# Nine column groups of the adaptive modulation: partition sums moved from TensorE to VectorE's 32x32 transpose and row sums

## The reference

```
sc  = silu(c);  scc = silu(c_ctx)
mod_l = sc  @ ada_w[i] + ada_b[i]        # 6 x 1024 values for the latent tokens
mod_c = scc @ ada_w[i] + ada_b[i]        # 6 x 1024 values for the context tokens
sh1, s1, g1, sh2, s2, g2 = split(mod, 6)
```

## Time and profile before

| | |
|---|---|
| median of 3 runs | 1933.3 us (1932.83 to 1934.34) |
| the profiled execution | 1933.96 us, its span from first to last instruction 1932.1 us |
| mean granted TensorE clock | 0.999 |
| PE busy | 1921.8 us, 99% of the span |
| PE weight loads busy | 1653.0 us, 86% |
| DVE busy | 1371.3 us, 71% |
| ACT busy | 674.7 us, 35% |
| POOL busy | 381.2 us, 20% |

### The profile page before, as it was taken

The page is one execution under the profiler, slowest core; times in us unless marked ns, Lnnn a source line. Parts: engine busy times, 40 slices in busy tenths (PEclk is TensorE's granted clock), DMA queues, the critical chain, the costliest instruction groups (busy, mean ns, idle before and its releaser), DMA issues.

```text
span 1932.1 us, 24878 instructions
## 1 busy us (share of the span) xinstructions
PE 1921.8 (99%) x9432; PEld 1653.0 (86%) x9432; DVE 1371.3 (71%) x1977; ACT 674.7 (35%) x936; POOL 381.2 (20%) x364
## 2 busy tenths in 40 slices
PE   9999999999999999999999999999999999999998
PEld 6889899899889988998888888888888888888887
DVE  3756587698887777767887755754764787777778
ACT  2423122145323222331546225324413443434443
POOL 0300312313211222222310130130030037110004
PEclk9999999999999999999999999999999999999999
DMA  9623334345998998898596285366447525977656
GB/s 327 262 70 67 120 121 131 106 135 134 210 230 216 215 230 231 229 236 226 175 223 240 88 251 181 129 192 197 151 144 231 173 90 178 246 210 194 175 146 148
DMA packets 120419, 350.59 MB, mean 181 GB/s; under 512 B 17520, under 2 KB 30448, under 8 KB 115568
## 3 DMA queue, kind: packets, MB, share of 16 engines
q1 hardware_dynamic: 91200, 268.11, 40.9%
q0 software_dynamic: 27280, 77.08, 22.2%
q10 hardware_dynamic: 1824, 3.85, 0.6%
HBM read 296.01 MB, written 40.92 MB: 174 GB/s over the span
## 4 chain that ended last, share of the span: by engine, by line
PE 95%; POOL 1%; DMA 1%; DVE 1%; issue 1%; ACT 0%; SPq 0%; POOLq 0%; DVEq 0%; ACTq 0%
PE bank L1157 18%; PE bank L1159 18%; PE bank L1158 18%; PE bank L1195 4%; PE bank L1196 4%; PE bank L1197 4%; PE bank L1565 3%; PE bank L1564 3%; PE bank L1562 3%; PE bank L1626 3%; PE bank L1627 3%; PE bank L1624 3%; PE bank L1809 2%; PE bank L1808 2%; PE bank L1806 2%; PE bank L1468 1%
## 5 line engine op out<-in xcount | busy, mean ns | idle before, releaser
L2377 DVE TENSOR_TENSOR w_lo<-raw,w_hi 128x1024 fp32r<-128x1024 f32 x132 | 168.8, 1282 | 170.8 <-ACT w_hi L1832 170.6
L1832 ACT ACTIVATE w_hi<-raw 128x1024 fp32r<-128x1024 f32 x132 | 139.2, 1055 | 279.3 <-PE bank L1159 158.9
L1157 PE MATMUL bank<-w_hi,act_hi 128*128 128x512 f32 x504 | 198.2, 393 | 0.0
L1159 PE MATMUL bank<-w_hi,act_lo 128*128 128x512 f32 x504 | 196.4, 390 | 0.0
L1158 PE MATMUL bank<-w_lo,act_hi 128*128 128x512 f32 x504 | 196.3, 390 | 0.0
L1157 PE MATMUL bank<-hT_hi,w_hi 128*128 128x384 f32 (+2 forms) x544 | 191.8, 353 | 0.0
L1158 PE MATMUL bank<-hT_lo,w_hi 128*128 128x384 f32 (+2 forms) x544 | 190.8, 351 | 0.0
L1159 PE MATMUL bank<-hT_hi,w_lo 128*128 128x384 f32 (+2 forms) x544 | 190.8, 351 | 0.0
L1195 PE MATMUL bank<-w_hi,hT_hi 128*128 128x512 f32 x336 | 131.0, 390 | 0.0
L1196 PE MATMUL bank<-w_lo,hT_hi 128*128 128x512 f32 x336 | 130.8, 389 | 0.0
L1197 PE MATMUL bank<-w_hi,hT_lo 128*128 128x512 f32 x336 | 130.7, 389 | 0.0
(11 more groups left out here) (458 smaller groups left out, 4858.2 us busy)
## 6 DMA issues: line engine op xcount, KB each, us to landing
raw<-w_units_d SPq DMA_DIRECT2D x234, 512.0 KB, 4.6
mod<-mod_units_d SPq DMA_DIRECT2D x64, 384.0 KB, 4.5
wsum<-w_units_d SPq DMA_DIRECT2D x44, 512.0 KB, 4.5
raw<-weight_sums_d SPq DMA_DIRECT2D x32, 512.0 KB, 4.4
wsum<-w_units_d POOLq DMA_DIRECT2D x25, 512.0 KB, 7.9
wsum<-wsum POOLq DMA_DIRECT2D x19, 512.0 KB, 7.0
bv<-mod_units_d SPq DMA_DIRECT2D x16, 512.0 KB, 3.6
weight_sums_d<-w_units_d POOLq DMA_DIRECT2D x8, 1024.0 KB, 12.4
```

The costliest lines, as they stand in the source:

```text
L1157: nc.tensor.matmul(out, s_hi, m_hi, start=first, stop=False)
L1159: return nc.tensor.matmul(out, s_lo, m_hi, start=False, stop=last)
L1832: nc.scalar.activation(halves_of(phase, k, i)[0], raw[:, s, :], ACT.Copy).then_inc(hi_done, 1)
L2377: tt(lo, raw[:, s, :], f32(hi), ALU.subtract).then_inc(lo_done, 1)
```

## The change

In the nine places the sum over partitions goes to DVE. `nc.vector.transpose` transposes every 32x32 block of the tile by itself, so that in each quarter of 32 partitions a row sum over 32 neighbouring values is the sum over the quarter's 32 partitions for one column. Two instructions for each 128x1024 tile (`part_sum`): the transpose into a scratch tile, and a `tensor_reduce` to 128x32; in the MLP each tile goes in two halves of 384 columns. TensorE then adds the four quarters and sets the sums in their partitions with four small matmuls (`part_columns`): the weights are `sel32`, four 32x32 unit matrices one under another (made once, in `v`), the moving operand has 16, 12 or 6 columns, and each writes 32 partitions of bank 7. DVE adds the bias from there (`add_part_bias`).

The places move. `vz`: DVE sums between its first and second `split_lo`, TensorE's matmuls where the transposes were. `gmlp`: DVE sums between the last two `split_lo` of `down`, that is behind the drains of half 0; TensorE's matmuls behind the second tile of the last sweep; the bias behind DVE's second drain of half 1. `ffn0`: DVE sums in one place behind `products(4)`; TensorE's matmuls behind the fifth tile of the last sweep; the bias behind the fifth drain of half 1. Step `rows` and ACT's copy are gone in all nine. The first product of the next group waits for DVE's own count `small_done` in place of TensorE's step.

```diff
-_VZ = _V[:2] + [("rows2", 6, "A")] + _V[2:3] + [("cols2", 7, "D")] + _V[3:]
+_VZ = _V[:3] + [("cols2", 7, "D")] + _V[3:]
-_DOWN0M = _DOWN0[:1] + _ROWS + _COLS + _DOWN0[1:]
+_DOWN0M = _DOWN0[:10] + _COLS + _DOWN0[10:]
-_DOWN0S = _DOWN0[:8] + _ROWS + _DOWN0[8:10] + _COLS + _DOWN0[10:]
+_DOWN0S = _DOWN0[:13] + _COLS + _DOWN0[13:]
...
+            def part_columns(phase, i, label, n, vectors):
+                sums = part_sums_v if phase == "vz" else part_sums
+
+                pe.wait_ge(small_done, sums_made(phase, i))
+                free(phase, i, label)
+                for q in range(4):
+                    src = sums[:, 0:vectors, 0:4 * n].rearrange("p v (j q) -> p q j v", q=4)[:, q]
+                    last = nc.tensor.matmul(bank[7][32 * q:32 * q + 32, 0:n * vectors].rearrange("p (j v) -> p j v", v=vectors),
+                                            sel32[:, :], src, start=True, stop=True, tile_position=(0, 32 * q))
+                last.then_inc(pe_step, 1)
...
                 token_units(phase, i, 0, "v", TILES0, {} if phase == "v" else {
-                    (1, 5): sums_2, (2, 5): lambda: mod_columns("vz", 0, 2, rbuf[:, 0, :], 7)})
+                    (2, 5): lambda: part_columns(phase, i, "cols2", 8, 2)})
...
-                    down(phase, i, CH, TILES0, act_hi0, act_lo0, ready, rows=rows, columns=columns)
+                    down(phase, i, CH, TILES0, act_hi0, act_lo0, ready,
+                         columns1=lambda: part_columns(phase, i, "cols0", 8, 2))
...
-                    down(phase, i, 7, TILES0, act_hi0, act_lo0, ready, rows1=rows, columns1=columns)
+                    down(phase, i, 7, TILES0, act_hi0, act_lo0, ready, after=TILES0 - 2,
+                         columns1=lambda: part_columns(phase, i, "cols0", 6, 2 if p < PIECES_MIXED else 1))
...
-                    mod_rows(phase, i, 0, rows1[:, 0:6] if p >= PIECES_MIXED else rows1[:, :], 6, begin)
...
                     products(4)
+                    group1_sum(p, 0)
+                    group1_sum(p, 1)
+                    group1_sum(p, 2)
+                    group1_sum(p, 3)
                     block0_lo(p + 1, 0)
                     drain0(p, 1, 0)
                     drain0(p, 1, 1)
-                    mod1_columns(phase, i)
                     for t in range(2, TILES0 - 1):
                         drain0(p, 1, t)
                         products(5, t - 2)
+                    add_part_bias(phase, i, "cols0", 1, 6 * i, 6, 2 if p < PIECES_MIXED else 1)
...
+            def part_sum(done, v, a, src, turned, sums=part_sums):
+
+                n = src.shape[1] // 32
+                dve.wait_ge(small_done, done)
+                nc.vector.transpose(turned, src).then_inc(small_done, 1)
+                dve.wait_ge(small_done, done + 1)
+                nc.vector.tensor_reduce(sums[:, v, a:a + n], turned.rearrange("p (n r) -> p n r", r=32),
+                                        mybir.AxisListType.X, ALU.add).then_inc(small_done, 1)
...
+                if n == 2:
+                    dve.wait_ge(mod0_used, KC)
+                    for v in range(2):
+                        part_sum(7 + 2 * v, v, 0, sums_v[v], stage[:, :, :].rearrange("p a b -> p (a b)"), part_sums_v)
...
+                    def group_sums():
+                        dve.wait_ge(mod0_used, KC * (p + 1))
+                        for v in range(2):
+                            part_sum(sums_made(phase, i) - 4 + 2 * v, v, 0, sums_g[v], stage[:, :, :].rearrange("p a b -> p (a b)"))
```

More of the change, by code:

```diff
@@ L353, in build @@
         lg = sb("lg", [P, 5, 8])
+        part_sums = bst[:, :, :, :].rearrange("p a b c -> p (a b c)")[:, 0:64].rearrange("p (v n) -> p v n", v=2)
+        sel32 = sb("sel32", [P, 32])
         ADAB, LNC, BU, LNG, LNB = 0, 96, 160, 176, 192
@@ L790, in build, with sums_made @@
         ws_half = [wsT[:, 4 * h:4 * h + 4, :].rearrange("p a b -> p (a b)") for h in range(2)]
+        def sums_made(phase, i):
+            done = 11
+            if phase == "vz":
+                return done
+            if phase == "gmlp":
+                return done + 4 * (i + 1)
+            return done + 4 * (PIECES_A - 2) + 8 * min(i + 1, PIECES_MIXED) + 4 * max(0, i + 1 - PIECES_MIXED)
         block = keep.enter_context(nc.Block())
@@ L1202, in token_units, with down @@
                             between[q, t]()
-            def down(phase, i, k0, tiles, a_hi, a_lo, ready, late=None, rows=None, columns=None, rows1=None, columns1=None):
+            def down(phase, i, k0, tiles, a_hi, a_lo, ready, late=None, columns1=None, after=1):
                 for half in range(2):
@@ L1254, in down @@
                                     last.then_inc(pe_step, 1)
-                                    if t == 1 and columns1:
+                                    if t == after and half == 1 and columns1:
                                         columns1()
@@ L1258, in down @@
                                 last.then_inc(pe_step, 1)
[L1259 to L1262, removed]
             def down_blocks(phase, k0, order, a_hi, a_lo, ready, ln_phase=None, late=None, rows=None, columns=None):
@@ L1567, in ffn0 @@
                         last.then_inc(pe_step, 1)
[L1569 to L1576, removed]
-                def rows():
[L1579 to L1584, removed]
+                def rows():
+                    pe.wait_ge(mod_used, len(MOD1_SEQ))
+                    mod_sums(phase, i, "rows0", 6, [sum1(p), sum1(PIECES_F - 1, 1)], WIDE_M1 // 2)
                 def columns():
-                    if phase == "ffn0" and p >= PIECES_MIXED:
-                        column_sums("cols0", 7, 1)
-                        return
                     mod_columns(phase, i, 0, rows1, 7)
@@ L2127, in _ @@
                 if phase != "gmlpz":
-                    down_splits(phase, i, CH, copy if p else None)
+                    down_splits(phase, i, CH, None)
                 else:
@@ L2633, in ffn0, with down @@
                     split_lo("heads", 0, 1)
-            def down(phase, i, k0, tiles, then=None):
+            def down(phase, i, k0, tiles, then=None, sums=None, columns=None):
                 if phase not in ("heads", "ffn1a"):
@@ L2643, in down @@
                 split_lo(phase, i, k0 + 3)
+                if sums:
+                    sums()
                 if phase == "ffn1a":
@@ L2649, in down @@
                     drain(phase, i, 1, t, tiles)
+                    if t == 1 and columns:
+                        columns()
             C11, C12, Z57, NEG21, NEG16 = range(5)
@@ L2917, in product, with add_part_bias @@
                 last.then_inc(used, 1)
+            def part_sum(done, v, a, src, turned, sums=part_sums):
[5 more added lines that the diff above has]
+                                        mybir.AxisListType.X, ALU.add).then_inc(small_done, 1)
+            def add_part_bias(phase, i, label, layer, c, n, vectors):
+                dve.wait_ge(pe_step, step_of(phase, i, label))
+                src = bank[7][:, 0:n * vectors].rearrange("p (j v) -> p j v", v=vectors)
+                if vectors == 1:
+                    src = src.to_broadcast([P, n, 2])
+                bias = cols[:, ADAB + 48 * layer + c:ADAB + 48 * layer + c + n].unsqueeze(2).to_broadcast([P, n, 2])
+                tt(modc[:, layer, c:c + n, :], src, bias, ALU.add).then_inc(dve_drain, 1)
             def product_v(n):
@@ L2933, in product_g @@
                 elif m:
-                    dve.wait_ge(pe_step, step_of("gmlp", m // KC - 1, "cols0"))
+                    dve.wait_ge(small_done, sums_made("gmlp", m // KC - 1))
                 product(sums_g, units_g[m % SLOTS_G], m % KC, 2, mod0_used)
@@ L3044, in _, with group_columns @@
                 if phase != "gmlpz":
[L3045 to L3049, removed]
+                    def group_sums():
+                        dve.wait_ge(mod0_used, KC * (p + 1))
+                        for v in range(2):
+                            part_sum(sums_made(phase, i) - 4 + 2 * v, v, 0, sums_g[v], stage[:, :, :].rearrange("p a b -> p (a b)"))
+                    def group_columns():
+                        add_part_bias(phase, i, "cols0", 0, 8 * (2 + p), 8, 2)
+                    if p:
+                        down(phase, i, CH, TILES0, lambda: normalise_v(p + 1), group_sums, group_columns)
+                    else:
+                        down(phase, i, CH, TILES0, lambda: normalise_v(p + 1))
                 else:
@@ L3063, in mod_product @@
                 elif g:
-                    dve.wait_ge(pe_step, step_of("ffn0", g - 1 if g <= PIECES_MIXED else g - 2, "rows0"))
+                    dve.wait_ge(small_done, sums_made("ffn0", g - 1 if g <= PIECES_MIXED else g - 2))
                 unit = mod1[:, n % SLOTS_M1, :]
@@ L3072, in mod_product, with group1_sum @@
                 last.then_inc(mod_used, 1)
+            def group1_sum(p, n):
+                vectors = 2 if p < PIECES_MIXED else 1
+                if n >= 2 * vectors:
```

(9 more changed lines are left out.)

42 lines of the change are left out of this document (19 added, 23 removed).

## The result

The kernel with the change takes 1940.26 us (median of 6 runs, 1939.42 to 1942.72), the kernel before 1933.07 beside it (6 runs): a ratio of 1.0037, 95% interval 1.0025 to 1.0050. The forecast was 1923.6 and faster; the kernel is 7 us slower, 16.7 us above the forecast.

What follows compares the result with a forecast made beforehand. PE's instruction stream was taken as the bound, with DVE's new work hidden. Removing 12.9 us and adding 3.15 left 9.7 us gained: 1933.3 - 9.7 = 1923.6 us, range 1921.4 to 1928.8.

Steps and rivals of the forecast that it cites:

- TensorE's terms: On PE in the nine places: 12.9 us of removed work goes, 3.15 us of small matmuls comes, 9.7 us gained.
- The price of an insertion: PE time added by four small matmuls at each of nine places: 0.35 us, bounds 0.11 to 0.89.
- Rival C: In the nine places the small matmuls run one behind another: 0.89 us each, 8.0 in all, 1928.4; chance 0.08.
- VectorE's terms: DVE's transposes and reductions take 1.25 us at 1024 columns, 0.58 at 384; some 36 us more, all hidden.
- D: DVE's transpose needs several cycles per four-byte element; at 4.9 us each the kernel is slower by 8.7, 1942; chance 0.06.
- cover: Time by which DVE's sums are done before PE needs them: 0.9 us in gmlp, 3.6 in ffn0's pieces 0 to 2.
- B: In gmlp DVE's sums come late, both transposes at 2.36 us: 2.8 us given back, 1926.4; chance 0.14.
- E: Freed PE time doesn't reach the end because a transfer or DVE's normalisation chain sets a later stage: 1933; chance 0.08.

## Why the prediction was wrong

**The step that failed is one that the sum doesn't have.** The forecast takes PE's instruction stream as the time and prices what is taken out and put in; everything that stays it leaves at 0.227 us from start to start. It gives no reason why that pace should stay. sel32 comes into it only as the weights of the small matmuls. That it is also a tile, and that 128 bytes of it move the operands of thousands of matmuls against each other, was priced by no term and no rival. The missed term is 17.2 us: the kernel after less the same kernel with sel32 inside bst, 1940.26 - 1923.04; alone in the kernel before the tile costs 16.2. By the starts of both traces about 9.8 of it arise between 160 and 1040 us and 8.5 behind that; the sum of 18.3 is higher because the two traces differ by 1.9 the other way before 60 us, and their executions aren't the median ones.

**TensorE's terms were right.** With sel32 out of the way, the same matmul's start less that of the kernel before, us:

```
start before        60     160     240     300     380     520     600     720     840     920    1040    1900
sel32 in bst     -0.29   -1.58   -1.58   -2.84   -4.13   -4.15   -5.12   -7.05   -9.02  -10.04  -10.48  -10.44
```

vz brings 1.29, gmlp 1.26 and 1.29 (forecast 1.65 - 0.35 = 1.30 each); ffn0's first piece 0.97 (forecast 1.32 - 0.35), all six 5.9. From 60 to 920 us it is 9.75; the forecast's sum was 9.7. That close a hit is partly luck: what the insertions cost more than the forecast, 0.3 us in all (below), came off again in small amounts at the same places. Some 0.4 more come between 920 and 1040 us, where nothing was edited, and 0.3 before 60.

**The price of an insertion** is 0.397 us in vz, 0.392 in gmlp, 0.388 and 0.378 in ffn0, where 0.35 was taken from a line through 512 and 384 columns: within the bounds (0.11 to 0.89), 0.3 us more over nine places. Rival C, 0.89, falls. The timeline of TensorE in gmlp's first piece, sel32 inside bst:

```profile
293.78 0.39 PE L1171 MATMUL bank<-w_lo,act_hi 128*128 128x512 f32 x1
294.01 0.39 PE L1172 MATMUL bank<-w_hi,act_lo 128*128 128x512 f32 x1
294.33 0.26 PE L1376 MATMUL bank<-bst 128*32 128x16 f32 x8
294.52 0.50 PE L1170 MATMUL bank<-w_hi,act_hi 128*128 128x512 f32 x1
294.85 0.39 PE L1171 MATMUL bank<-w_lo,act_hi 128*128 128x512 f32 x1
```

From the last start ahead to the second behind, 294.008 to 294.854, less 0.454. Eight records end within 0.26 us. The page that spoke against the tiling (the Trainium skill, TensorEngine Tiling (Array Packing), Instruction Overhead) gave 0.53 for a place by estimate; 0.39 lies nearer to the line than to it.

**VectorE's terms were right too.** Its timeline in the same piece of the same kernel:

```profile
288.50 1.23 DVE L2928 STREAM_TRANSPOSE stage<-vtok 128x1024 f32<-128x1024 f32 x1
289.76 1.22 DVE L2930 TENSOR_REDUCE bst<-stage 128x32 f32<-128x1024 f32 x1
291.02 1.25 DVE L2928 STREAM_TRANSPOSE stage<-vtok 128x1024 f32<-128x1024 f32 x1
292.30 1.22 DVE L2930 TENSOR_REDUCE bst<-stage 128x32 f32<-128x1024 f32 x1
293.44 1.22 DVE L2374 TENSOR_TENSOR w_lo<-raw,w_hi 128x1024 fp32r<-128x1024 f32 x1
```

Transposes take 1.23 to 1.25 us (forecast 1.25 with the gap), so D falls. The 1942 that it named for a transpose of 4.9 us is near the measured 1940, but only by chance. The sums are done at 293.52, TensorE's matmuls start at 294.33: a cover of 0.8 where the forecast had 0.9, so B falls; ffn0's pieces 0 to 2 have 3.1 (forecast 3.6). In the MLP, by line and form over the kernel after:

```profile
L2928 DVE STREAM_TRANSPOSE rows<-macc x18: 572/578/579, 570.8 to 886.8; 128x384 f32<-128x384 f32 x18
L2930 DVE TENSOR_REDUCE bst<-rows x18: 553/553/554, 571.4 to 887.4; 128x12 f32<-128x384 f32 x18
```

1240 ns at 1024 columns and 578 at 384 make 1.03 ns for an element and lane. The Trainium skill's Vector Engine (DVE) Microarchitecture Reference, section 3.8, has one element per cycle and lane, by the prediction's estimate 1.07 us for 1024, or 1.04 ns each; the slope bears it out. All new passes add up to 35.1 us (6 x 2.46 + 18 x 1.13; forecast 36); busy time rose by 31, since the other passes took 2 less in all, and stretches in which a pass overlaps its neighbour, as at 293.44, count once there.

**E falls**: with sel32 inside bst the freed 10 us reach the end (-10.48 us at 1040, -10.44 at 1900).

## What to carry to other kernels

Where TensorE is the bound, as here, a new tile is a change to every matmul whose two operands it parts: give it a size that keeps the operands' places against each other (here a multiple of 256 bytes per partition), or put it into room that is already there. After any change that allocates, compare the mean of the same matmul by pair of tiles before and after: here 395 in place of 389 ns for some pairs, with no wait beside it, was the sign. A price list of what a change adds and removes isn't complete without what it moves in memory.

## What the runs showed of the hardware

The distance of successive fp32r 128x512 matmuls depends on the place of the streaming operand against the weights, counted round 256 bytes per partition as far as 0, 64, 128, 192 and 256 bytes show: 227 ns when both are in step, as in the kernel before, up to 233 when not, and not alike in both directions (64 bytes cost 18.8 us in this kernel, 192 cost 8.0). By the sizes in the source the tiles from hT to lg add up to a multiple of 256 bytes, so if they lie one behind another as allocated, the pairs of the kernel before all start at the same place in that count. Moving all tiles together by 128 bytes costs nothing. No record is named as waited for, and a weight load keeps its 187 to 189 ns in the slow pairs as in the fast ones.

That a matmul's stream and the load of the next weights, which run at the same time, get into each other's way would fit. The places where one pair of tiles follows another speak for it in part. In the kernel after, from 100 us on, there are 38 places where a matmul's own operands are not parted, but its streaming tile and the next matmul's weights are: the next one starts 232.7 ns behind. In 22 places where only the next matmul's own operands are parted it starts 226.5 ns behind. But with 64 and 192 unused bytes the 38 places stand at 226 ns too, and behind a parted run the first matmuls are slow with nothing parted any more. Which two reads meet, and why in step they don't, stays open.
